# Order of the first weight chunks in a hybrid decoder step: the first projection chunk is loaded third, and its products run in two halves around the last two modulation chunks

## What is computed

```python
mod = (jax.nn.silu(c) @ w_mod + b_mod)[:, None, :]          # w_mod: 1024 x 6144
sh_a, sc_a, gt_a, sh_f, sc_f, gt_f = jnp.split(mod, 6, axis=-1)
h = rms_norm(x, g_mix) * (1.0 + sc_a) + sh_a
p = h @ w_in                                                # 1024 x 4104
rq, rk, rv, rg, mqk, mv, mo, mi, mf = jnp.split(p, cuts, axis=-1)
```

## Time and profile before

| | |
|---|---|
| Median of 3 runs | 1337.64 us (1332.58 to 1338.12) |
| Profiled execution | 1335.96 us, its span 1334.1 us |
| TensorE busy | 1201.8 us (90% of the span) |
| DVE, ACT, POOL busy | 386.8, 221.7, 66.1 us |
| Mean granted clock of TensorE | 0.959 of full speed |
| Read from HBM | 458.35 MB, 348 GB/s over the span |

### The profile page before, as it was taken

The page is one execution under the profiler, slowest core; times in us unless marked ns, Lnnn a source line. Parts: engine busy times, 40 slices in busy tenths (PEclk is TensorE's granted clock), DMA queues, the critical chain, the costliest instruction groups (busy, mean ns, idle before and its releaser), DMA issues.

```text
span 1334.1 us, 23252 instructions
## 1 busy us (share of the span) xinstructions
PE 1201.8 (90%) x8796; PEld 558.3 (42%) x8797; DVE 386.8 (29%) x850; ACT 221.7 (17%) x369; POOL 66.1 (5%) x148
## 2 busy tenths in 40 slices
PE   5999999899799999987899998899778998997895
PEld 4655557555444344432344442344232343332352
DVE  0173214736522213221222231122122221221136
ACT  3012232012212112111111111101111111111111
POOL 1010000314000000000000000000000000000002
PEclk9999999979799999998999999899988998998998
DMA  9937234685269999999999999999999999999992
GB/s 374 350 126 266 91 121 190 185 296 200 101 253 412 422 422 420 422 421 422 422 421 421 375 423 421 423 421 392 421 422 422 422 422 422 422 421 423 421 422 105
DMA packets 79956, 465.62 MB, mean 349 GB/s; under 512 B 8594, under 2 KB 26326, under 8 KB 27826
## 3 DMA queue, kind: packets, MB, share of 16 engines
q1 hardware_dynamic: 76898, 458.87, 84.4%
q10 hardware_dynamic: 2640, 5.68, 1.3%
q0 software_dynamic: 384, 0.59, 0.2%
HBM read 458.35 MB, written 6.16 MB: 348 GB/s over the span
## 4 chain that ended last, share of the span: by engine, by line
PE 60%; DMA 21%; SPq 10%; DVE 4%; issue 2%; POOL 1%; ACT 1%; POOLq 0%; DVEq 0%; ACTq 0%
DMA mem<-in_w_up 19%; PE psum L969 16%; PE psum L1005 11%; SPq L406 10%; PE psum L1015 8%; PE psum L625 6%; PE psum L940 4%; PE psum L606 3%; PE psum L812 2%; DMA mem<-in_mod_chunks 2%; PE psum L629 2%; PE psum L462 1%; PE psum L733 1%; PE psum L1037 1%; PE psum L979 1%
## 5 line engine op out<-in xcount | busy, mean ns | idle before, releaser
L969 PE MATMUL psum<-mem 128*32 128x512 f32 (+2 forms) x2432 | 412.2, 635 | 80.2 <-DMA mem<-in_w_up 70.7
L969 PEld LDWEIGHTS psum<-mem 128*32 128x32 f32 (+2 forms) x2432 | 115.8, 123 | 368.6 <-issue 199.1
L1005 PE MATMUL psum<-mem 128*32 128x512 f32 (+3 forms) x1024 | 214.1, 594 | 0.0
L1979 DVE TENSOR_SCALAR mem<-psum 128x256 f32<-128x256 f32 (+3 forms) x32 | 19.2, 601 | 592.2 <-PE psum L973 592.2
L1015 PE MATMUL psum<-mem 128*128 128x512 f32 (+1 forms) x396 | 156.9, 607 | 3.1 <-issue 1.4
L1998 DVE TENSOR_TENSOR mem<-mem,psum 128x1024 f32<-128x1024 f32 (+1 forms) x96 | 100.4, 1045 | 98.6 <-PE psum L1015 98.6
L1005 PEld LDWEIGHTS psum<-mem 128*32 128x32 f32 (+3 forms) x1024 | 82.7, 127 | 104.2 <-issue 93.7
L1340 ACT ACTIVATE mem<-mem 128x256 f32<-128x256 f32 (+3 forms) x32 | 17.9, 559 | 420.8 <-DVE mem L1979 420.8
L940 PEld LDWEIGHTS psum<-mem 128*128 128x128 bf16 x2304 | 78.5, 98 | 18.7 <-issue 18.4
L625 PE MATMUL psum<-mem 128*128 128x512 f32 x192 | 84.2, 595 | 0.0
L940 PE MATMUL psum<-mem 128*128 128x64 bf16 (+1 forms) x2304 | 82.4, 197 | 0.0
(11 more groups left out here) (262 smaller groups left out, 813.6 us busy)
## 6 DMA issues: line engine op xcount, KB each, us to landing
mem<-in_w_up SPq DMA_DIRECT2D x256, 1024.0 KB, 25.3
mem<-in_w_down SPq DMA_DIRECT2D x128, 1024.0 KB, 18.3
mem<-in_mod_chunks SPq DMA_DIRECT2D x12, 2048.0 KB, 12.1
mem<-in_in_chunks SPq DMA_DIRECT2D x8, 2048.0 KB, 8.8
mem<-in_out_chunks SPq DMA_DIRECT2D x2, 2048.0 KB, 9.7
mem<-in_x_prompt ACTq DMA_DIRECT2D x2, 1024.0 KB, 7.1
mem<-in_state_ret SPq DMA_DIRECT2D x4, 512.0 KB, 6.6
mem<-in_state_mlstm_c SPq DMA_DIRECT2D x4, 512.0 KB, 9.5
```

The source lines that it names most:

```text
L969: last = pe.matmul(out, xg[:, c, cols], moving, start=(c == 0), stop=False)
L1005: last[c] = pe.matmul(psum[slots * q:slots * q + slots, 6 + u, :], turned, piece_slot(UP + c, 2, D)[:, piece % 2, 512 * u:512 * u + 512], ...
```

## The change

The chunks mod2 and mqk0 move to the second and third place of the loads, mod1 and mod3 to the fourth and fifth. mod3 shares a slot with mod0 now, and mqk0 has the slot that mqk1 is to take after it. TensorE computes mod2 where mod1 was, transposes modT0 and modT2, and DVE modulates slices 0 to 3 from them. TensorE then does the products of mqk0 on these four slices, for all four column groups, into four open banks; then mod1 and mod3 into banks 6 and 7, their transposes into the same banks, and, when DVE has modulated slices 4 to 7, the other half of the products of mqk0. mqk0's four results are evacuated after modT3.

```diff
-        CH = (["mod0", "mod1", "mod2", "mod3", "mqk0", "mod4", "mqk1", "mod5", "rq", "mod10", "rk", "mod11",
+        CH = (["mod0", "mod2", "mqk0", "mod1", "mod3", "mod4", "mqk1", "mod5", "rq", "mod10", "rk", "mod11",
...
-        OUTS = ["c", "mod0"] + [f"xnT{k}" for k in range(4)] + ["mod1"] + [f"xnT{k}" for k in range(4, KD)]
-        OUTS += ["par", "nstate", "mod2", "modT0", "modT1", "mod3", "modT2", "modT3"]
-        for n in range(4, 16):
+        OUTS = ["c", "mod0"] + [f"xnT{k}" for k in range(4)] + ["mod2"] + [f"xnT{k}" for k in range(4, KD)]
+        OUTS += ["par", "nstate", "modT0", "modT2", "mod1", "mod3", "modT1", "modT3"]
+        OUTS += [f"mqk0_{m}" for m in range(4)]
+        for n in range(5, 16):
...
+        BANK = {n: q % BANKS for n, q in Q.items()}
+        BANK.update(mod1=6, mod3=7, modT1=6, modT3=7)
...
-            mod_rows("mod1", 1)
+            mod_rows("mod2", 1)
...
-            mod_rows("mod2", 2)
             mod_transposed(0)
+            mod_transposed(2)
+
+            def qk_products(w, m, ks):
+
+                for k in ks:
+                    pe.wait_ge(S("h_ready"), k + 1)
+                    last = pe.matmul(psum[:, BANK[f"mqk0_{m}"], 0:NTOK], w[:, k, 128 * m:128 * m + 128], hT[:, k, :],
+                                     start=(k == 0), stop=(k == KD - 1))
+                return last
+
+            w = take_chunk(2)
+            pe.wait_ge(S("evacuated"), Q["mod1"])
+            for m in range(4):
+                qk_products(w, m, range(4))
+            mod_rows("mod1", 3)
+            mod_rows("mod3", 4)
             mod_transposed(1)
-            mod_rows("mod3", 3)
-            mod_transposed(2)
             mod_transposed(3)
-            for n in range(4, 16):
+            for m in range(4):
+                last = qk_products(w, m, range(4, KD))
+                if m < 3:
+                    last.then_inc(S("projected"), 1)
+            last.then_inc(used[2], 1)
+            pe.wait_ge(used[2], 1)
+            pe.nop().then_inc(S("projected"), 1)
+            for n in range(5, 16):
...
-            def modulate():
-
-                step(STT(coefA, modT[:, 8:16, :], 1.0, parT[:, :, 5:6].to_broadcast([128, KD, 9]), ALU.add, ALU.mult))
+            def modulate(ks):
+
+                n = len(ks)
+                part = slice(ks[0], ks[-1] + 1)
...
+            dve.wait_ge(S("evacuated"), Q["modT2"] + 1)
+            modulate(range(4))
             dve.wait_ge(S("evacuated"), Q["modT3"] + 1)
-            modulate()
+            modulate(range(4, KD))
```

More of the change, by code:

```diff
@@ L470, in mod_rows @@
             def mod_rows(name, n):
-                q = Q[name]
-                bank_free(q)
+                if BANK[name] < BANKS:
+                    bank_free(Q[name])
                 pe.wait_ge(S("brow_in"), 16)
-                mod_product(n, q % BANKS, brow).then_inc(S("projected"), 1)
+                mod_product(n, BANK[name], brow).then_inc(S("projected"), 1)
             def late_mod_rows(j):
@@ L482, in mod_transposed @@
             def mod_transposed(n):
-                q = Q[f"modT{n}"]
-                bank_free(q)
+                if BANK[f"modT{n}"] < BANKS:
+                    bank_free(Q[f"modT{n}"])
                 pe.wait_ge(S("evacuated"), Q[f"mod{n}"] + 1)
-                pe.transpose(psum[:, q % BANKS, 0:128], modr[:, n, :], ident).then_inc(S("projected"), 1)
+                pe.transpose(psum[:, BANK[f"modT{n}"], 0:128], modr[:, n, :], ident).then_inc(S("projected"), 1)
             def cumulate():
@@ L603, in _ @@
                         for k in range(KD):
-                            if n == 4 and m == 0:
-                                pe.wait_ge(S("h_ready"), k + 1)
                             last = pe.matmul(psum[:, q % BANKS, 0:NTOK], w[:, k, 128 * m:128 * m + 128], hT[:, k, :],
@@ L1091, in bq @@
             def bq(name):
-                return Q[name] % BANKS
+                return BANK[name]
             act.wait_ge(S("zeroed"), 1)
@@ L1115, in _ @@
                 evac_input(k)
-            evac_mod(1)
+            evac_mod(2)
             for k in range(4, KD):
@@ L1120, in _ @@
             evac("nstate", [(nT[:, 0, :], psum[:, bq("nstate"), 0:32])])
-            evac_mod(2)
             evac_modT(0)
+            evac_modT(2)
+            evac_mod(1)
+            evac_mod(3)
             evac_modT(1)
-            evac_mod(3)
-            evac_modT(2)
             evac_modT(3)
@@ L1145, in _ @@
             DST = {"rq": rq, "rk": rk, "rv": rv, "rg": rg, "mo": mo}
-            for n in range(4, 16):
+            for n in (2, *range(5, 16)):
                 name = CH[n]
@@ L1552, in _ @@
                     .then_inc(S("xn_ready"), 1)
-            def modulate():
-                step(STT(coefA, modT[:, 8:16, :], 1.0, parT[:, :, 5:6].to_broadcast([128, KD, 9]), ALU.add, ALU.mult))
+            def modulate(ks):
+                n = len(ks)
+                part = slice(ks[0], ks[-1] + 1)
                 def seqs(v):
-                    return v[:, :, SEQ:NTOK].rearrange("p k (b t) -> p k b t", b=NSEQ)
+                    return v[:, part, SEQ:NTOK].rearrange("p k (b t) -> p k b t", b=NSEQ)
                 def cols(v):
[L1562 to L1566, removed]
+                    return v.unsqueeze(3).to_broadcast([128, n, NSEQ, TS])
+                step(STT(coefA[:, part], modT[:, 8 + ks[0]:9 + ks[-1], :], 1.0,
+                         parT[:, part, 5:6].to_broadcast([128, n, 9]), ALU.add, ALU.mult))
+                step(TT(seqs(hT), seqs(xnT), cols(coefA[:, part, 1:9]), ALU.mult))
+                shift = cols(modT[:, part, 1:9])
+                for i, k in enumerate(ks):
+                    TT(seqs(hT)[:, i], seqs(hT)[:, i], shift[:, i], ALU.add)
                     TSC(hT[:, k, 0:SEQ], xnT[:, k, 0:SEQ], coefA[:, k, 0:1], modT[:, k, 0:1], ALU.mult, ALU.add)\
                         .then_inc(S("h_ready"), 1)
+            dve.wait_ge(S("evacuated"), Q["modT2"] + 1)
+            modulate(range(4))
             dve.wait_ge(S("evacuated"), Q["modT3"] + 1)
-            modulate()
+            modulate(range(4, KD))
             dve.wait_ge(S("evacuated"), Q["mqk1_3"] + 1)
```

## The result

The changed kernel takes 1346.76 us (median of 6 runs, 1344.33 to 1348.86), the kernel before 1337.82 us beside it (6 runs, 1332.58 to 1338.2): ratio 1.0073, 95% interval 1.0054 to 1.0092, so 8.9 us slower by the medians. The profiled execution took 1346.85 us, its span 1345.0.

The account below looks back on a forecast made before the run. TensorE, nearly always at work in the opening, was taken to bound it, with delays reaching the end. Opening -1.0, clock +1.7, stall +6.2, clock behind it +1.7: +8.6 on 1335.96, 1344.6, raised to 1345 us (1339 to 1350).

Parts of the forecast that it names:

- First product at 28.6: Start of mqk0's first half: first product at 28.6 us, with TensorE idle 1.6 us before it.
- Second half 2.4 us behind mod3: mqk0's second half: starts at 44.2 us, 2.4 us after mod3's end at 41.8, and ends at 53.0.
- the opening gains 1.0 us at full clock: Up to mqk0's last product: ends at 53.0 us instead of 54.04, -1.0 us without clock falls.
- The clock in the two gaps: Gaps before mqk0's two halves: one clock fall taken between them, +1.7 us, making the opening +0.7.
- The load of mqk1: mqk1's load, issued after mqk0 frees its slot: lands after 8.7 us, ends 7.8 and 9.3.
- The stall: TensorE's wait before mqk1's products: 8.7 us landing less 2.5 us of mod4's product, +6.2 us (5.3 to 6.8).
- The clock behind the stall: mqk1's products after the wait: one clock fall, +1.7 us (0 to 2.5).
- The whole passes on to the end: From 57 us to the first expert at 352 us: the whole +8.6 us reaches the end.
- A: Rival: all three gaps lower the clock and the load lands late, +11.6 us, 1347.5 us; chance 0.22.
- B: Rival: the clock holds in both gaps and behind the stall, 1340.3 to 1341.2 us; chance 0.19.
- C: Rival: mqk1's load is hidden or the expert stream swallows the delay, -1.0 us, 1335 us; chance 0.08.
- D: Rival: later clock falls move, one or two of 1.7 us spared or added; chance 0.06 as deciding.

Follow-up runs that it names:

- swap_and_fill_in_after: Changed kernel with mqk1 loaded sixth, mod4 seventh, and three unused products in each gap before mqk0's halves; ratio 0.9984 to the kernel before.
- hold_in_before: Kernel before with one more wait: mqk1's load is issued only when mqk0's last product is done; ratio 1.0052, median 1343.07 us.
- swap_in_after: Changed kernel with mqk1 loaded sixth and mod4 seventh, so that mod4 waits for mqk0's slot; ratio 1.0032 to the kernel before.
- fill_stall_in_after: Changed kernel with ten unused products (5.4 us) behind mod4's product, keeping TensorE busy until mqk1 lands; ratio 1.005 to the kernel before.
- before_look_2: Kernel before, unchanged, profiled a second time; 1335.7 us of device time.
- before_look_4: Kernel before, unchanged, profiled a fourth time; 1336.63 us of device time.
- before_look_3: Kernel before, unchanged, profiled a third time; 1334.12 us of device time.

## Why the prediction was right

The forecast was 1345 us (1339 to 1350) and slower with 0.66; measured were 1346.8 and 1346.2. The sum gave +8.6 us to the end of the opening; the medians moved by 8.9 and 10.2, mqk1's end in the trace by 10.8. The mechanism was right: the load that waits for the slot, the stall, the low clock behind it. That 8.6 stands so close to 8.9 is in part luck: measured by the trace the opening was +2.5 for +0.7, the stall 5.8 for 6.2 and the clock behind it 2.5 for 1.7, and these add up to 2.2 us more than was forecast. Step by step:

- *First product at 28.6*: 28.66, with 1.76 us idle in front of it (1.6 said). *mod1 and mod3 without a wait for DMA, 2.2 us each*: so it was (39.15 and 41.38). *Second half 2.4 us behind mod3*: 43.62 to 45.97, 2.35 us, of which 0.79 are transposes (1.56 idle). The prediction called all 2.4 a gap. That the opening gains 1.0 us at full clock is nearly what swap_and_fill_in_after shows: 53.52 for 54.04, in an execution that was 0.3 us behind already at the transposes (26.80 for 26.46 in the profile above), so 0.8 us.
- *The clock in the two gaps* was the term mis-sized: one fall taken, two came, each at 1.7 to 1.8 us (10.56 and 10.59 for 8.8 at full clock by the sum, 8.87 and 8.90 measured with the gaps filled). The opening ended at +2.5, not +0.7. Both falls came in all five profiles with unfilled gaps in front of the halves.
- *The load of mqk1*: 8.7 us said, 8.3 measured. The stall 6.2 said, 5.76 measured. (The upper end of the landing, 7.8 and twice 0.7, is 9.2, not 9.3.) hold_in_before makes it in a kernel without a split, swap_in_after takes it away: shown from both sides.
- *The clock behind the stall*: 1.7 said with 0 to 2.5 as ends, 2.46 measured (20.00 for 17.54), and shown to be the clock by fill_stall_in_after.
- *The whole passes on to the end*: 11.1 us at the first expert, 8.9 and 10.2 in the medians; right in the main, but that the whole passes on is not shown. I had it from the 52 GB/s in the earlier trace rows.

Of the rivals, A (every gap lowers the clock) is what the traces show, with the short landing instead of the late one. Its sum without the late landing is -1.0 + 5.0 + 6.2 + 0.8 = +11.0; the +10.2 in the prediction leaves out the 0.8 as well. The trace says 10.8, so A's mechanism, given 0.22, fits better than the forecast's one fall in two. The rule of the Trainium skill (TensorE: Matmul & The Clock Gate, HAM oscillation) that stood beside it is about a wait for DMA. The one such gap, in front of mqk1, agrees with it: 5.76 us idle, then products at 0.50. The two others were waits for DVE of 1.76 and 1.56 us, and the clock fell there too. B (the clock holds) and C (load hidden or delay swallowed) did not happen. The row that was weighed against A, the gap at 254 us without a fall, is one outcome of two: the same gap fell in before_look_2. And D, later falls that move, is what the four profiles of the kernel before show of the same program from one execution to the next. So a single row of a gap without a fall says little.

One reading of the prediction stays unproven: that mod0's products were slow (3.64 us for 1.96) because of the clock. The granted clock reads 1.00 there; see the last section.

## What to carry to other kernels

In a ring of slots a chunk that is used in two halves holds its slot from the first half to the end of the second. Ask which load is to take that slot, and when it is needed: here that one load went from 6 us of slack to 5.8 us of stall, while the products that were brought forward had hardly any idle time to fill. Cutting one wait into two also makes two places where TensorE's clock can fall; a few unused products in an unavoidable gap gave 0.2% here (interval 0.04% to 0.39%), and the reordering with the same filling gave no more.

## What the runs showed of the hardware

The price of a low clock behind a stall does not follow from the length of the stall. Idle 5.92 us cost 1.6 us behind it, 5.76 us cost 2.46, 5.96 us cost 2.69 and 7.67 us cost 1.46 (19.15, 20.00, 20.23 and 19.00 us for 17.54). What counts is how much of the low stretch lies inside the idle time: it ran from 59.0 to 65.8, from 63.1 to 69.9, from 63.8 to 70.6 and from 63.0 to 69.9 us in the four (by the clock in stretches of 0.5 us), and the products began at 62.5, 64.9, 65.1 and 66.9. That leaves 3.3, 5.0, 5.4 and 3.0 us of them at the low clock, and half of that is what they lost. Why the clock fell 2.4 us into one of these idle stretches and 3.8 to 4.6 us into the others is open.

The same gap of TensorE can lower the clock in one execution and not in the next: 1.86 us at 254 us did in before_look_2 and before_look_4, and did not in the first profile and before_look_3.

The granted clock reads 1.00 from the start of the record to 35 us, yet mod0's 64 instructions (15.06 to 18.70 us) took 3.64 us where later ones of the same shape took 1.96. A lower clock that the column doesn't show would fit, but no run here tells it from another cause. So a column of 1.00 before its first change is to be held against the durations.
